# First batch in groups of two tiles, and the v-row sums moved to the second batch's stages

## The reference

```
h  = rmsnorm(x) @ W_in  -> pool | q | k | v | gate_pool | gate_attn
x += (sigmoid(gate_pool) * (pool_mixer(p) @ W_pool_out)
      + sigmoid(gate_attn) * (attention(q, k, v) @ W_attn_out)) @ W_out
h  = rmsnorm(x)
for 8 heads: two scores with 128 keys each, top 16 of each, top 16 of the 256 sums
             -> 128 experts per token: idx, gate = softmax(top scores)
a   = h . expert_u[idx]                 # 128 rows of 1024 per token
x  += (gelu(a) * gate) . expert_v[idx]  # 128 rows of 1024 per token
y  = rmsnorm(x)
```

## Time and profile before

| | us |
|---|---|
| median of 3 runs | 3017.53 (3012.39 to 3021.62) |
| the profiled execution | 3016.6 |
| its span in the profile | 3014.8 |
| PE busy | 2622.4 (87%) |
| VectorE busy | 2071.7 (69%) |
| POOL busy | 1531.1 (51%) |
| ScalarE busy | 483.9 (16%) |

### The profile page before, as it was taken

How to read it: one execution, slowest core, us unless ns; L and a number is a source line. 1 busy time by engine, 2 the same in 40 slices (tenths; PEclk the granted TensorE clock), 3 DMA queues, 4 the chain that set the end, 5 groups by cost and what they waited for, 6 DMA issues and landing times.

```text
span 3014.8 us, 30618 instructions
## 1 busy us (share of the span) xinstructions
PE 2622.4 (87%) x9973; PEld 1508.8 (50%) x9973; DVE 2071.7 (69%) x4568; ACT 483.9 (16%) x910; POOL 1531.1 (51%) x1284
## 2 busy tenths in 40 slices
PE   7999868879978888875689889898998999989998
PEld 6785546535734465443344445454444454445444
DVE  1337876685098758557678967976666776767867
ACT  2311601120135013222220000110000000000001
POOL 0002674455455740223527776676775665656754
PEclk9999989999999999898899999999999999999999
DMA  4376897698788974556879999999999999999997
GB/s 153 112 238 220 268 389 281 250 328 285 272 298 254 378 270 162 201 213 256 304 253 403 384 399 394 368 397 399 383 401 387 393 404 391 387 372 401 402 400 306
DMA packets 362209, 961.55 MB, mean 319 GB/s; under 512 B 28000, under 2 KB 152672, under 8 KB 359008
## 3 DMA queue, kind: packets, MB, share of 16 engines
q0 software_dynamic: 184320, 671.17, 59.1%
q1 hardware_dynamic: 173152, 259.52, 24.6%
q10 hardware_dynamic: 4608, 29.36, 2.4%
HBM read 930.58 MB, written 29.36 MB: 318 GB/s over the span
## 4 chain that ended last, share of the span: by engine, by line
PE 56%; DMA 20%; issue 10%; DVE 8%; ACT 3%; POOL 2%; another core or an unknown queue 0%; DVEq 0%; ACTq 0%; SPq 0%; POOLq 0%
PE bank L616 16%; PE o_bank L883 14%; DMA wslot<-in_expert_uT 14%; PE bank L893 13%; PE bank L604 5%; PE o_bank L633 3%; DMA ring<-in_expert_v,idx 3%; DMA ring<-in_expert_u,idx 2%; POOL ring L1234 2%; PE bank L669 2%; DVE ring L1269 2%; DVE consts L1640 2%; ACT region_s L1035 1%; DVE neg_max L1358 1%; DVE consts L1634 1%
## 5 line engine op out<-in xcount | busy, mean ns | idle before, releaser
L1234 POOL DMA_INDIRECT ring<-in_expert_u,idx x640 | 809.9, 1265 | 729.5 <-DVE idx L1541 315.6
L1234 POOL DMA_INDIRECT ring<-in_expert_v,idx x640 | 721.0, 1127 | 731.7 <-PE o_bank L633 391.4
L1269 DVE CUSTOM_DVE_ANT_0 ring<-ring,h 128x1024 f32<-128x1024 f32 x640 | 761.8, 1224 | 120.5 <-DMA ring<-in_expert_u,idx 112.0
L883 PE MATMUL o_bank<-region_b,wslot 128*128 128x384 f32 x2048 | 706.1, 500 | 96.4 <-DMA wslot<-in_expert_uT 94.5
L893 PE MATMUL bank<-wslot,gate_attn 128*128 128x512 f32 x1536 | 684.8, 596 | 12.9 <-DVE gate_attn L1577 12.4
L883 PEld LDWEIGHTS o_bank<-region_b,wslot 128*128 128x128 f32 x2048 | 399.7, 196 | 411.2 <-DMA wslot<-in_expert_uT 104.9
L1286 DVE SCALAR_TENSOR_TENSOR region_a<-ring,dots,region_a 128x1024 f32<-128x1024 f32 x384 | 492.8, 1284 | 53.6 <-DMA ring<-in_expert_v,idx 23.2
L893 PEld LDWEIGHTS bank<-wslot,gate_attn 128*128 128x128 f32 x1536 | 292.8, 191 | 358.2 <-issue 310.4
L1141 ACT ACTIVATE gate_attn<-o_bank 128x384 f32<-128x384 f32 x128 | 62.7, 490 | 1341.1 <-PE o_bank L883 1240.4
L633 PE MATMUL o_bank<-ring,gate_attn 128*32 128x512 f32 x1024 | 146.9, 702 | 108.2 <-DMA ring<-in_expert_v,idx 102.1
L616 PE MATMUL bank<-region_b,wslot 128*128 128x128 f32 (+2 forms) x768 | 231.9, 460 | 2.8 <-ACT region_b L929 2.8
(11 more groups left out here) (171 smaller groups left out, 1907.1 us busy)
## 6 DMA issues: line engine op xcount, KB each, us to landing
wslot<-in_expert_uT SPq DMA_DIRECT2D x128, 512.0 KB
wslot<-in_expert_v SPq DMA_DIRECT2D x128, 512.0 KB
wslot<-in_w_in SPq DMA_DIRECT2D x34, 1024.0 KB
wslot<-in_w_query SPq DMA_DIRECT2D x24, 1024.0 KB
expert_weights<-region_p ACTq DMA_DIRECT2D x24, 1024.0 KB
wslot<-in_w_out SPq DMA_DIRECT2D x12, 1024.0 KB
region_s<-expert_weights SPq DMA_DIRECT2D x8, 1536.0 KB
region_p<-expert_weights SPq DMA_DIRECT2D x8, 1536.0 KB
```

Source lines behind the costliest of these rows:

```text
L883: ins = nc.tensor.matmul(dense_in[q][:, 0:DENSE_T], u_cols[slot][:, k, :], h2T[:, k, T - DENSE_T:T], start=(k == 0), stop=(k == KD - 1))
L1234: nc.gpsimd.indirect_dma_start(ring[:, n % RING, :], None, expert_u if what == "u" else expert_v, bass.IndirectOffsetOnAxis(ap=ids, axis=0 ...
L1269: nc.vector.tensor_tensor_reduce(row, row, h2[:, H2_AT[k], :], 1.0, 0.0, ALU.mult, ALU.add, dots[:, DOTS_AT[k] + s:DOTS_AT[k] + s + 1]).th ...
```

## The change

Group 0 becomes tiles 0 and 1 of batch 0, group 1 tiles 2 and 3. The gather order becomes: u0 whole, the first 96 rows of u1, then in turn eight rows of v0 and four of u1, then the rest of v0, then v1. No quad of v rows stands in group 1 or in batch 1's projections any more: the first eight of v0 stand behind the eight `out` jobs of group 2, the other 24 in its query steps c = 0 to 3, 24 of v1 in c = 4 to 7 (one behind the first and third quarter step, two behind the second and fourth), and the last eight behind `h2D` and six w jobs. On DVE merge(0, 0) and (0, 1) no longer share their places with (0, 2) and (0, 3): merge(0, 2) stands behind group 2's attention, merge(0, 3) between its `attn_out` and its `out`. Dots stand inside the merges and inside `rotate(1)`. Core of the diff:

```diff
-GROUP_OF = ((0, (0,)), (0, (1, 2, 3)), (1, (0, 1, 2, 3)))
+GROUP_OF = ((0, (0, 1)), (0, (2, 3)), (1, (0, 1, 2, 3)))
-GATHERS = [("u", 0), ("v", 0), ("u", 1), ("v", 1), ("u", 2), ("u", 3), ("u", 4), ("v", 2), ("v", 3), ("v", 4)]
-ROW = {key: n * SLOTS for n, key in enumerate(GATHERS)}
+def gather_order():
+    rows = lambda what, k, first, last: [(what, k, s) for s in range(first, last)]
+    yield from rows("u", 0, 0, SLOTS)
+    yield from rows("u", 1, 0, U_BEFORE)
+    for n in range((SLOTS - U_BEFORE) // 4):
+        yield from rows("v", 0, 8 * n, 8 * n + 8)
+        yield from rows("u", 1, U_BEFORE + 4 * n, U_BEFORE + 4 * n + 4)
+    yield from rows("v", 0, (SLOTS - U_BEFORE) * 2, SLOTS)
+    yield from rows("v", 1, 0, SLOTS)
+    for what in "uv":
+        for k in range(EARLY, len(GATHERED)):
+            yield from rows(what, k, 0, SLOTS)
+U_BEFORE = 96
-SUMS_AT = {("query", 1, 4): 2, ("query", 1, 5): 2, ("query", 1, 6): 2, ("query", 1, 7): 2, ("hT",): 2,
-           **{("gate_pool", d): 1 for d in range(KD)},
-           **{("p", c, tp): 1 for c in range(2) for tp in range(2)}, ("pooled",): 2,
-           **{("q", c, tp): 1 for c in range(2) for tp in range(2)}, ("kv", 0): 1, ("kv", 1): 3}
-LATE_SUMS_AT = {**{("query", 2, c): 3 for c in range(2, 8)}, ("h2D",): 4, ("chosen",): 2, **{("w", n): 1 for n in range(67, 96, 4)}}
+SUMS_AT = {**{("out", c, tp): 1 for c in range(4) for tp in range(2)},
+           **{("query", c, step): 1 + step % 2 for c in range(4) for step in range(4)}}
+LATE_SUMS_AT = {**{("query", c, step): 1 + step % 2 for c in range(4, 8) for step in range(4)},
+                ("h2D",): 2, **{("w", n): 1 for n in range(67, 88, 4)}}
@@ vector engine, main stream
             merge(0, 0)
-            pool_out(1, 1)
+            pool_out(1)
             attention(1, 1)
-            attn_out(1, 6)
-            out(1, 3)
+            attn_out(1, 3)
+            out(1, 4)
             dot(4)
             norm2(1)
             for hp in range(HALVES):
                 top_halves(1, hp)
-                if hp < 5:
-                    dot(4)
-                if hp == 5:
-                    weigh(0)
+                dot(1)
             norm1(1)
-            merge(0, 1)
-            merge(0, 2)
+            dot(24)
+            merge(0, 1, lambda: dot(2))
+            dot(SLOTS - dotted[0])
             turn_ids(2, 1)
-            merge(0, 3)
-            rotate(1)
-            pool_out(2, 2)
-            add_sums(0)
+            rotate(1, 2)
+            weigh(0)
+            pool_out(2, 1)
+            attention(2, 1)
+            filled(dve, 2, "probsT", len(attention_steps(2)) - 1)
+            merge(0, 2, lambda: dot(2))
+            attn_out(2, 2)
+            softmax(2)
             split_ids(0)
-            attention(2, 1)
-            attn_out(2, 6)
-            out(2, 4)
+            merge(0, 3, lambda: dot(1))
+            out(2, 2)
             norm2(2)
-            weigh(1)
             for c in range(HALVES // 2):
                 for step_ in range(4):
                     for n in early_weights(c, step_):
                         one_hots(n)
                     if c and step_ < 2:
                         top_halves(2, 2 * c - 2 + step_)
+                    if c < 2:
+                        dot(min(2, EARLY * SLOTS - dotted[0]))
+                if c == CHOSEN_AFTER - 1:
+                    softmax(3)
+                    split_ids(1)
+                    dot(EARLY * SLOTS - dotted[0])
+                if c == CHOSEN_AFTER:
+                    weigh(1)
+                if c == TURN_AFTER:
+                    add_sums(0)
```

More of the change, by code:

```diff
@@ L175, in jobs_of @@
     if g == LAST_GROUP[1]:
-        yield (g, "chosen", 0), None
+        yield (g, "wT", 0), None
     for c in range(KD // 2):
@@ L194, in jobs_of @@
                     yield (g, "w", n), None
-        if WT_AFTER.get(g) == c:
-            yield (g, "wT"), None
+        if g == LAST_GROUP[1] and c == CHOSEN_AFTER:
+            yield (g, "chosen", 1), None
+        if g == LAST_GROUP[1] and c == TURN_AFTER:
+            yield (g, "wT", 1), None
     if g == LAST_GROUP[1]:
@@ L452, in all_used @@
         def all_used(eng, key):
-            for n in range(ROW[key] + SLOTS - RING, ROW[key] + SLOTS):
+            last = {}
+            for s in range(SLOTS):
+                last[ROW[(*key, s)] % RING] = ROW[(*key, s)]
+            for n in last.values():
                 used(eng, n)
@@ L625, in sum_rows @@
                 k, quads = SUMS_OF[key]
+                if k and quads[0] == 0:
+                    pe.wait_ge(sums_added, k)
                 for r in quads:
-                    rows = [ROW["v", k] + QUARTERS * r + q for q in range(QUARTERS)]
+                    rows = [ROW["v", k, QUARTERS * r + q] for q in range(QUARTERS)]
                     for n in rows:
@@ L840, in builds @@
                             build_weights(n)
+                        sum_rows("query", c, step)
                 for c in range(HALVES // 2):
@@ L1081, in stores @@
                             store_weights(n)
+                        weigh_sums("query", c, step)
                 for c in range(HALVES // 2):
@@ L1092, in queries, with take_weights, gate_exp @@
                         stores(c, 2 + hp % 2)
-                    if g == LAST_GROUP[0] and c == WT_AFTER[g] - 1:
-                        gelu(0)
-                    if WT_AFTER.get(g) == c:
-                        k = g - 1
-                        move(dots[:, DOTS_AT[k]:DOTS_AT[k] + SLOTS], (g, "wT"), view=lambda bank: bank[:, 0:SLOTS])
-                    weigh_sums("query", g, c)
-            def gate_exp(b, tiles, merges):
-                act.wait_ge(top_ready, merges)
-                g = gate[:, b, tiles, :]
+                    if g == LAST_GROUP[1] and c == CHOSEN_AFTER - 1:
+                        gate_exp(3)
+                    if g == LAST_GROUP[1] and c == CHOSEN_AFTER:
+                        take_chosen(1)
+                        gelu(1)
+                    if g == LAST_GROUP[1] and c == TURN_AFTER:
+                        take_weights(1)
+            def take_weights(k):
+                move(dots[:, DOTS_AT[k]:DOTS_AT[k] + SLOTS], (LAST_GROUP[1], "wT", k), view=lambda bank: bank[:, 0:SLOTS])
+            def gate_exp(n):
+                b, t = MERGED[n]
+                act.wait_ge(top_ready, n + 1)
+                g = gate[:, b, t, :]
                 nc.scalar.activation(g, g, ACT.Exp).then_inc(top_exp, 1)
@@ L1164, in group @@
                 if g == LAST_GROUP[1]:
-                    take_chosen(0)
+                    take_weights(0)
                 gates(g)
                 if g == LAST_GROUP[1]:
-                    take_chosen(1)
+                    gate_exp(2)
+                    take_chosen(0)
+                    weigh_sums("out", 0, 0)
+                    for c in range(D // CHUNK):
+                        for tp in tile_pairs(g):
+                            filled(act, g, "out", c, tp)
+                            weigh_sums("out", c, tp[0] // 2)
                 norm2(g)
-                if g == LAST_GROUP[1]:
-                    gelu(1)
                 queries(g)
@@ L1302, in norm1, with rotate @@
                                             ALU.mult).then_inc(xr_ready, 1)
-            def rotate(b):
+            def rotate(b, rows=0):
                 if b == 0:
@@ L1311, in rotate @@
                         moved(dve, FIRST_GROUP[b], "kv", t // 2)
-                    qk = qkv[:, t, 0:Q_W + KV_W]
+                    dot(rows)
+                    qk = qkv[b][:, t, 0:Q_W + KV_W]
                     link(nc.vector.tensor_tensor(rope1, qk, qk, ALU.mult))
@@ L1392, in attn_out @@
                     dot(rows)
-                    if g == LAST_GROUP[1] and d == KD // 2:
-                        split_ids(1)
                     moved(dve, g, "gate_attn", d)
@@ L1711, in _ @@
             merge(1, 3)
-            softmax(1, slice(3, 4))
+            softmax(4)
             split_ids(2)
@@ L1716, in _ @@
             add_sums(1)
-            norm2_again(4)
+            for k in AGAIN:
+                norm2_again(k)
             pauses = iter(range(8))
```

174 lines of the change are left out of this document (75 added, 99 removed).

## The result

The changed kernel takes 3179.6 us, the median of four runs (3169.7 to 3197.3), against 3016.1 us before. The ratio is 1.055, with a 95% interval of 1.049 to 1.060. The profiled execution took 3186.4 us and spans 3184.6. The forecast was 3118, with a range of 3040 to 3185: direction right, size 62 us short (68 against the profiled execution). The change costs 163 us and not the 101 of the sum.

The account below looks back on a forecast made before the run. Dense stage bound by transfers, its time carried over; before it, PE's waits decide. Groups -45, projections -27, gates +8, `out` +53, query steps +128, tail -17, extra norm +1: +101 on 3016.6 gives 3118 us, range 3040 to 3185.

Parts of the forecast that it names:

- gain of 45 us: Groups 0 and 1: two tiles each, with quads and their stalls gone, would end group 1 at 574, not 619.8.
- cross-check: All 512 gathered rows, at 2.5 us each from a first gather at about 368, would end at 1637.
- The query steps: Query steps of group 2: a loss of 128 us, 436 against 307.6, from six quads a step on the ring.
- D: Single quad behind the third quarter of query steps c = 2 to 7; claimed to wait 4.7 us.
- F: Second quad behind the fourth quarter of query steps c = 2 to 7; claimed to wait 4.7 us.
- E: First quad behind the fourth quarter of query steps c = 2 to 7; claimed to go without a wait.
- turn of 10.5 us: Gather ring: time until a used quad is replaced, read from the kernel before and used throughout the sum.
- upper bounds: Query steps c = 0 and 1: 84 and 73 us if every ring turn per eight rows is exposed; 70 each taken.
- (1): `out` and query steps: waits on the ring vanish and only bytes count, 40.5 us for c = 2 to 7; 2998 us, chance 0.10.
- (2): `out` and query steps: rows at full rate are no limit, every step takes 36.6 us; 2935 us, chance 0.03.
- (3): Before `out`: merges, dots and rotate on DVE hold PE, shrinking the 72 us won to 20; 3170 us, chance 0.22.
- (4): Whole kernel: the change doesn't do what it says and nothing moves; 3017 us, chance 0.05.

Follow-up runs that it names:

- experiment 7: Changed kernel with the old grouping back (group 0 one tile, group 1 three) and some DVE dots placed thinner; ratio 1.048 to the kernel before.
- experiment 9: Kernel of experiment 8 plus the groups of two, v0's quads all in batch 1's projections and dots strewn to match; 3054.5 us, ratio 1.010.
- Experiment 6: Changed kernel with every 1 MB store of dense weights made twice, the second to an unread buffer; 3217.6 us in a single run.
- experiment 5: Changed kernel with a ring of six places, not eight, same rows in the same order; 3329.0 us in a single run.
- experiment 1: Changed kernel with the quads of query steps c = 2 to 7 standing 2, 2, 1, 1 behind the quarters, not 1, 2, 1, 2; ratio 1.040.
- Experiment 2: Changed kernel with all u1 rows gathered ahead of v0 and their dots moved into attn_out, merge(0, 3) and out; ratio 1.037.
- experiment 8: Kernel before with only its v1 quads spread: one behind each quarter of query steps c = 1 to 7, four behind h2D; 2989.3 us, ratio 0.986.

## Why the prediction was right, and where its size failed

**The first part was right.** Group 1 ends at 571 (574 forecast), attention starts at 809.0 (805), `out` at 979.3 (976). PE's wait for the ids is 22.3 us (17). The "gain of 45 us" in groups 0 and 1 is there in the trace, and it comes from the quads and dots that left this stretch, which the prediction names. The expectations of experiments 7 and 9 took it for the worth of the groups of two, and that failed: with the old grouping group 1 ends just as early (experiment 7), and without the rest of the change the groups of two, with v0's quads packed closer for them, cost 75 us before the dense stage (1563.4 against 1488.0, experiment 9). The prediction did see that the first gather comes at 368 (it was 367.7), but used it only in the cross-check.

**`out` was right.** The first two quads wait 6.65 and 11.83 us (12 and 14 forecast), and the stage with its sums takes 115 us (112). Part of this agreement is luck: all waits on rows come to 32 us where the sum had 39.5, and work to 83 where it had 72, since quads after a wait take up to 3.64 us here too. The 3 us that the issues beside merge(0, 3) might have cost do not show: between 1000 and 1014 us POOL issues one row per pause, each released by a dot, in 0.94 us. In order of time on PE:

```profile
994.73 3.64 PE L657 MATMUL o_bank<-ring,gate_attn 128*32 128x512 f32 x16 [6.65 <-DMA ring<-in_expert_v,idx]
...
1018.06 3.64 PE L657 MATMUL o_bank<-ring,gate_attn 128*32 128x512 f32 x16 [11.83 <-DMA ring<-in_expert_v,idx]
```

**The query steps: mechanism right, term too small by 53 us.** This is the step that failed. From the first query product at 1116.0 to the last sums behind c = 7 at 1605.3 it took 489 us; the forecast was 436.
- For c = 2 to 7 it took 55.4 us a step and not 49.4, 36 us in all. The letters held: D and F wait, E does not, a quad after a wait takes 3.64 us. The step of the sum that was too small is F's wait, taken at 4.7 us like D's: it is 8.4 to 14.0 us, 10.2 in the mean, 33 us over the sum in six steps. D waits 6.1 in the mean, 8 us over it in six steps; in c = 2 PE has 2.9 us of work in front of it and not 3.9. All else in the six steps is 5 us shorter than the sum. The turn of 10.5 us was read where only gathered rows moved in its last 6 us; it holds for D (10.9 us from B's end) and not for F (15.7), with which a load and a store pass. A duration that holds a transfer had been carried over as a constant. Experiment 6 shows the dependence (3.9 us a step for 2.1 MB more), experiment 5 shows the ring as the limit, experiment 1 shows that the place of the pairs is worth 7 us a step.
- For c = 0 and 1 it took 156.7 us and not 140. That the upper bounds add up to 157 is luck: they were 84 and 73, and the steps took 73.8 and 82.9, the second 10 us over its bound. The 18.8 us of one dot are more than a whole turn of 10.5 us. Experiment 2 takes the u rows out of this place: the two steps shrink by 44 us to 113, the dense stage starts 45 us earlier.

A row of the kernel before would have shown the longer turn. It is the quad at the end of the last query step, where the first loads of the dense stage and a store pass. POOL's last issue for it stands at 1407.92, 12.8 us before its start:

```profile
1420.71 3.33 PE L633 MATMUL o_bank<-ring,gate_attn 128*32 128x512 f32 x16 [15.20 <-DMA ring<-in_expert_v,idx]
```

**The tail** took 89 us (100 forecast); the w jobs follow each other in about 1.9 us where DVE is not held up (one-hots at 1640.48 and 1642.35), not in 2.0. **The dense stage** took 1490 and not 1474, which is put down to the spread between executions. Together: -45 - 27 + 8 + 53 + 128 - 17 + 1 was +101. Against that: 3 us more before `out`, 7 more from there to the first query product (137 against 112 + 18), 53 in the query steps, 11 less in the tail. That gives the 52 us by which the dense stage came later than 1642; 16 more lie in the dense stage itself, and 52 + 16 is the 68 of the profiled execution.

**The rivals.** (1) "Transfers hide the latency" and (2) "PE-bound" are refuted: waits of 6 and 10 us in each step. The price of rival 1, 40.5 us a step by bytes, marks what could be had at best; 2, 2, 1, 1 reaches 47.9. (3) "DVE's order in the first part" wanted attention near 860; it was 809. The time of 3170 that this rival gave comes closer than the forecast, but for a reason that did not happen. (4) is refuted by the ratio. The cross-check, 2.5 us a row from the first gather, gave 1637 for the last sum, which ended at 1680.1: 512 rows at 2.56 us each. That it came this close is luck. Experiment 7 starts its gathers 98 us earlier and ends its sums only 15 us earlier than the changed kernel beside it. So the late first gather is not what loses the time in this kernel; the crowding of the v quads between `out` and the dense stage does, by the amounts above.

## What to carry to other kernels

A ring of N places with a turn T feeds at most N rows per T, and T is no constant: read it from a place where the same loads and stores pass beside the rows as in the new one, or give it a range that grows with these bytes. Spread the users of such a ring evenly over the work between them, so that no pair stands where little work follows. Do not let two engines alternate on it in short runs without a price for it, since each then waits for the other's places (44 us here). And ask of a later first gather what waits for its rows: 98 us cost nothing clear of noise where the v rows were used only from `out` on (experiment 7), while the version whose v0 had to pass ahead of attention started its dense stage 75 us later (experiment 9).

## What the runs showed of the hardware

The time from a quad's last issue to its first use was 6.0 us in the row of the kernel before and 6.0 to 6.4 for D in all six steps, with the DMA engines full (0.98 and 0.99 in the two stretches shown) but gathered rows almost alone, and 11.2 us with a 1 MB load and a 1 MB store beside them, at 383 GB/s and 1.03. The Trainium skill (DMA: Bandwidth & Descriptors, "Anatomy of one DMA — SWDGE (gpsimd) path"), by which the prediction weighed 3.2 us for one row alone, does not describe either case, since both have eight or more rows under way.

The dense stage was not touched by the size of the ring: 1482 us with six places, 1474 to 1500 with eight. At a DMA share of 0.99 two places fewer change nothing that can be seen, while at 0.78 they cost 13 us in every step.

PE's granted clock follows its waits: 0.98 over the steps of experiment 8, 0.90 with 2, 2, 1, 1, 0.85 in the changed kernel, 0.80 with a ring of six. A quad takes 1.92 us in unbroken work, and also after the 3.38 us wait of experiment 8; after the 6.25 us wait in the changed kernel it takes 3.64. The granted clock is 1.00 in the first two and 0.50 in the third, the 2.4 and the 1.2 GHz level. Short waits are not always free: after one of 3.00 us at 1343.29 in experiment 8 the quad took 3.21 us. So a wait can cost more than its length: the sums alone grew from 147 to 168 us.
